# Skip term and gate of a state-space stage per chunk, and its last branch products per half of their inputs

## What is computed

```python
cum = jnp.cumsum(ai, axis=1)                      # scan over chunks, forward and backward
y = jnp.einsum('btsg,btsge,bsgep->btgep', cb, Lm, xi)
y = y + jnp.einsum('btgn,bgenp->btgep', ci, S) * jnp.exp(cum)[..., None]
S_new = jnp.exp(cum[:, -1])[..., None, None] * S + jnp.einsum(...)
...
o_b = o_b + lp['d_skip'].reshape(SSM_GROUPS, SSM_HPG, 1) * xh      # the skip term
o_b = o_b.reshape(Bn, L, SSM_INNER) * jax.nn.silu(z)               # the gate
o_b = rms_norm_3(o_b.reshape(Bn, L, SSM_GROUPS, 512), norm_w)      # needs all of a group
y_b = o_b @ lp['w_pb']
merged = jax.nn.sigmoid(gate_a) * y_a + jax.nn.sigmoid(gate_b) * y_b
```

## Time and profile before

| | |
|---|---|
| median of 3 runs | 3487.12 us (3480.87 to 3489.39) |
| the profiled execution | 3491.64 us, of which its span is 3489.6 us |
| PE, DVE, POOL, ACT busy | 93%, 61%, 39%, 36% of the span |
| the stage | 2712 to 3054 us of the span |
| groups 0 to 3, end of the last `out` | 2773.1, 2857.9, 2927.3, 2999.7 us |

### The profile page before, as it was taken

The page is one execution under the profiler, slowest core; times in us unless marked ns, Lnnn a source line. Parts: engine busy times, 40 slices in busy tenths (PEclk is TensorE's granted clock), DMA queues, the critical chain, the costliest instruction groups (busy, mean ns, idle before and its releaser), DMA issues. The chain is left out here.

```text
span 3489.6 us, 44690 instructions
## 1 busy us (share of the span) xinstructions
PE 3258.9 (93%) x17806; PEld 2622.1 (75%) x17806; DVE 2117.2 (61%) x2504; ACT 1249.0 (36%) x1899; POOL 1371.3 (39%) x625
## 2 busy tenths in 40 slices
PE   8999998999998998999999999888989868899998
PEld 6778777888866677977888877767877646678886
DVE  6586865889865476354756554868982777631112
ACT  4233343323344332333423342334441654332222
POOL 3434343444432233435344433326641322334443
PEclk9999999999999999999999999999999979999999
DMA  3223353465333245444444222533333755422322
GB/s 120 91 85 125 123 172 131 168 233 179 132 113 97 79 132 156 129 164 156 148 145 151 96 98 88 176 97 125 105 113 115 231 156 151 154 85 83 106 92 76
DMA packets 237662, 451.26 MB, mean 129 GB/s; under 512 B 59936, under 2 KB 120032, under 8 KB 230416
## 3 DMA queue, kind: packets, MB, share of 16 engines
q1 hardware_dynamic: 230384, 437.93, 38.8%
q10 hardware_dynamic: 7072, 10.49, 0.8%
HBM read 396.88 MB, written 51.46 MB: 128 GB/s over the span
## 5 line engine op out<-in xcount | busy, mean ns | idle before, releaser
L288 POOL TENSOR_TENSOR stream_feed_lo<-stream_feed_raw,stream_feed_hi 128x1024 fp32r<-128x1024 f32 (+4 forms) x555 | 1255.8, 2265 | 2013.4 <-ACT stream_feed_hi L281 1959.5
L281 ACT ACTIVATE stream_feed_hi<-stream_feed_raw 128x1024 fp32r<-128x1024 f32 (+4 forms) x555 | 533.3, 963 | 707.5 <-PE ffn_low L188 174.9
L186 PE MATMUL shared_ps<-third_h_hi,stream_feed_hi 128*128 128x512 f32 (+1 forms) x776 | 322.1, 415 | 39.2 <-ACT third_in_rows_bend L794 17.1
L187 PE MATMUL shared_ps<-third_h_lo,stream_feed_hi 128*128 128x512 f32 (+1 forms) x776 | 311.3, 401 | 0.0
L188 PE MATMUL shared_ps<-third_h_hi,stream_feed_lo 128*128 128x512 f32 (+1 forms) x776 | 311.3, 401 | 0.0
L186 PE MATMUL mixer_acc<-first_h_hi,stream_feed_hi 128*128 128x512 f32 x544 | 222.2, 408 | 7.2 <-DVE first_h_lo L1406 5.4
L480 DVE SCALAR_TENSOR_TENSOR ffn_ada_sum<-ffn_ada_w,cond,ffn_ada_sum 128x512 f32<-128x512 f32 x196 | 219.0, 1134 | 4.1
L186 PEld LDWEIGHTS shared_ps<-third_h_hi,stream_feed_hi 128*128 128x128 f32 (+1 forms) x776 | 151.1, 195 | 85.6 <-issue 44.3
L188 PE MATMUL mixer_acc<-first_h_hi,stream_feed_lo 128*128 128x512 f32 x544 | 214.2, 394 | 0.0
L187 PE MATMUL mixer_acc<-first_h_lo,stream_feed_hi 128*128 128x512 f32 x544 | 214.1, 394 | 0.0
L186 PE MATMUL ffn_low<-ffn_mid_hi,stream_feed_hi 128*128 128x512 f32 x528 | 207.6, 393 | 4.7 <-DVE x_res L702 4.6
(11 more groups left out here) (767 smaller groups left out, 7243.0 us busy)
## 6 DMA issues: line engine op xcount, KB each, us to landing
stream_feed_raw<-in_stream SPq DMA_DIRECT2D x406, 512.0 KB, 3.4
ffn_ada_w<-in_w_ada SPq DMA_DIRECT2D x48, 1024.0 KB, 5.4
stream_feed_raw<-in_stream SPq DMA_DIRECT2D x50, 384.0 KB, 3.1
stream_feed_raw<-in_stream SPq DMA_DIRECT2D x52, 256.0 KB, 3.0
stream_feed_raw<-in_stream SPq DMA_DIRECT2D x36, 320.0 KB, 3.0
scratch_gates<-mixer_gate ACTq DMA_DIRECT2D x32, 256.0 KB, 2.1
mix_gin<-scratch_gates SPq DMA_DIRECT2D x32, 256.0 KB, 3.2
x_res<-scratch_cum SPq DMA_DIRECT2D x16, 512.0 KB, 7.6
```

What stands on the lines that cost most here:

```text
L186: nc.tensor.matmul(out, w_hi, x_hi, start=start, stop=False)
L187: nc.tensor.matmul(out, w_hi, x_lo, start=False, stop=False)
L281: self.nc.scalar.activation(self.hi[:, p % self.cut, :n], self.raw[:, p % self.deep, :n], ACT.Copy).then_inc(self.cut_hi, 1)
L288: eng.tensor_tensor(self.lo[:, p % self.cut, :n], self.raw[:, p % self.deep, :n], self.hi[:, p % self.cut, :n].bitcast(F32), ALU.subtract) ...
```

## The change

The skip term and the gate are done for chunk c of all four tiles at once: four instructions of 128 columns and one of 512, on data that `load_gate` fetches as 128 positions of 512 channels. On DVE, chunks 0 to 2 follow `out(g, 1)` to `out(g, 3)`, and chunk 3 closes the group. SP loads chunk 2 after e6 and chunk 3 after the next group's first `load_e`. `square` comes earlier on ACT, and `sums` on PE ahead of the six products. The last eight pieces become four pieces with the first half of the inputs of two column blocks each, and four with the second; eight sums are open at once, in eight banks, and the evictions follow `closed` (even blocks) or the spent piece (odd ones). SP loads all remaining weight pieces ahead of the gate rows. The diff, cut to its core:

```diff
@@ -3775,14 +3775,15 @@
-        self.cut, self.lesser, self.freed, self.gated = (s.sem(n) for n in ("cut", "lesser", "freed", "gated"))
+        self.cut, self.lesser, self.freed, self.gated, self.closed = (
+            s.sem(n) for n in ("cut", "lesser", "freed", "gated", "closed"))
...
-        return self.acc[:, q % 4 if q >= 2 * DT else q % 2]
+        return self.acc[:, (0, 1, 2, 3, 4, 6, 7, 5)[q - 2 * DT] if q >= 2 * DT else q % 2]

@@ -3814,34 +3815,30 @@
-    def tensor_last(self, pe, some, sums):
...
+    def tensor_last(self, pe, freeing, sums, before_sums):
+
+        def halves(part, m):
+            if m % 2 == 0:
+                self.w[0] = self.feed.take(pe, *self.pieces[2 * DT + DT // 2 * part + m // 2])
+            w_hi, w_lo = self.w[0]
             for k in range(DT // 2):
+                at, of = DT // 2 * part + k, DT // 2 * (m % 2) + k
+                if m == 0:
+                    self.wait_input(pe, 2 * DT, at)
+                last = product(self.nc, self.bank(2 * DT + m), (w_hi[:, of], w_lo[:, of]),
+                               (self.h[0][:, at], self.h[1][:, at]), at == 0, at == DT - 1)
+            if m % 2:
+                self.feed.spent(last)
+            elif part:
+                last.then_inc(self.closed, 1)
+
+        for m in range(DT):
+            if m == before_sums:
                 sums()
+            freeing(m)
+            halves(0, m)
+        for m in range(DT):
+            halves(1, m)

@@ -3865,7 +3862,13 @@
     def vector(self, dve, done):
         v = self.nc.vector
         for q in range(self.evicted, done):
-            self.feed.done(dve, *self.pieces[q])
+            m = q - 2 * DT
+            if m < 0:
+                self.feed.done(dve, *self.pieces[q])
+            elif m % 2:
+                self.feed.done(dve, *self.pieces[2 * DT + DT // 2 + m // 2])
+            else:
+                dve.wait_ge(self.closed, m // 2 + 1)
             dve.wait_ge(self.gate_in[q % 2], 16 * (q // 2 + 1))
             if q > DT:
                 dve.wait_ge(self.gated, q - DT)
@@ -3894,7 +3897,7 @@
-        y, xg, z = s.sb("y", [P, 4, T]), s.sb("xg", [P, 2, T]), s.sb("z", [P, 2, T])
+        y, xg, z = s.sb("y", [P, 4, T]), s.sb("xg", [P, 2, 4, P]), s.sb("z", [P, 2, 4, P])
@@ -3963,21 +3966,18 @@
-                def load_gate(g, j):
-                    n = 4 * g + j
+                def load_gate(g, c):
+                    n = 4 * g + c
                     if n >= 2:
                         sp.wait_ge(gated, n - 1)
-                    sp.dma_start(xg[:, j % 2], dram["xbc"][n * P:(n + 1) * P]).then_inc(xz_in[j % 2], 16)
-                    sp.dma_start(z[:, j % 2], dram["z"][Z3["z"] + n * P:Z3["z"] + (n + 1) * P]
-                                 ).then_inc(xz_in[j % 2], 16)
+                    for to, at in ((xg, dram["xbc"][T * g:T * (g + 1)]),
+                                   (z, dram["z"][Z3["z"] + T * g:Z3["z"] + T * (g + 1)])):
+                        sp.dma_start(to[:, c % 2], rows(at)[:, :, c * P:(c + 1) * P]).then_inc(xz_in[c % 2], 16)

                 for g in range(4):
                     dense.sync_gates(sp, pieces_by(g - 1, 1, 2) if g else 0)
                     dense.sync(sp, before(g, 0))
-                    if g:
-                        for j in range(2, 4):
-                            load_gate(g - 1, j)
-                    else:
+                    if g == 0:
                         load_x(0, 2)
                         load_x(0, 3)
                     for n in range(6, 8):
@@ -4004,6 +4004,7 @@
                     load_e(g, 6)
+                    load_gate(g, 2)
                     for n in range(2, 4 if g < 3 else 0):
                         load_cum(g + 1, n)
                     load_e(g, 7)
@@ -4012,15 +4013,16 @@
                         for n in range(4, 6):
                             load_cum(g + 1, n)
                         load_start(g + 1)
-                        for n in range(3):
-                            load_e(g + 1, n)
-                for j in range(2, 4):
-                    load_gate(3, j)
+                        load_e(g + 1, 0)
+                    load_gate(g, 3)
+                    for n in range(1, 3 if g < 3 else 0):
+                        load_e(g + 1, n)
                 sp.wait_ge(intra_ready, 28)
                 sp.dma_start(core.x[:], dram["x_keep"]).then_inc(x_back, 16)
+                dense.sync_gates(sp, 2 * DT)
+                dense.sync(sp, 3 * DT)
                 for q in range(2 * DT, 3 * DT):
                     dense.sync_gates(sp, q)
-                    dense.sync(sp, q)
                 sp.wait_ge(x_back, 16)

@@ -4089,6 +4091,9 @@
                         if j == 1:
                             fill(g, 0, 1)
                     fill(g, 0, 2)
+                    if g:
+                        pe.wait_ge(x_scaled, 8 * g + 8)
+                        sums(g - 1)
                     for n in range(6):
@@ -4100,8 +4105,6 @@
                             pe.wait_ge(advanced, 6 * g + n - 1)
-                        if n == 1 and g:
-                            sums(g - 1)
                         if d:
                             fill(g, 0, 3 + n // 2)
                     for c in range(4):
@@ -4132,8 +4135,20 @@
                         fill(g, 1, c)
-                pe.wait_ge(read, 30)
-                dense.tensor_last(pe, 1, lambda: (pe.wait_ge(y_made, 16), sums(3)))
+
+                def freeing(m):
+                    if m < 2:
+                        pe.wait_ge(dense.freed, 2 * DT - 1 + m)
+                    if m == 2:
+                        pe.wait_ge(read, 30)
+                    if m == 3:
+                        pe.wait_ge(read, 31)
+                    if m == 5:
+                        pe.wait_ge(y_made, 16)
+                    if m == 7:
+                        pe.wait_ge(meaned, 4)
+
+                dense.tensor_last(pe, freeing, lambda: (pe.wait_ge(y_made, 16), sums(3)), 2)

@@ -4151,8 +4166,8 @@

                 def square(g):
                     act.wait_ge(inter_ready, 4 * g + 4)
+                    act.wait_ge(gated, 4 * g + 4)
                     for j in range(4):
-                        act.wait_ge(gated, 4 * g + j + 1)
                         a.activation(squares[j], y[:, j], ACT.Square).then_inc(squared, 1)

                 def root(g):
@@ -4180,11 +4195,11 @@
                     for n in range(2 if g == 0 else 0):
                         decay(0, n)
                     dense.scalar(act, before(g, 0))
+                    if g:
+                        square(g - 1)
                     for n in range(2 if g == 0 else 3, 4):
                         decay(g, n)
                     dense.scalar(act, pieces_by(g, 0, 0))
-                    if g:
-                        square(g - 1)
                     dense.scalar(act, pieces_by(g, 0, 1))
                     for n in range(4, 6):
                         decay(g, n)
@@ -4201,8 +4216,9 @@
                         dense.scalar(act, pieces_by(g, 1, k))
                         if g < 3:
                             decay(g + 1, k)
+                dense.scalar(act, 2 * DT)
                 square(3)
-                dense.scalar(act, 2 * DT)
+                dense.scalar(act, 2 * DT + 1)
                 root(3)
                 high_parts(3)
                 for q in range(2 * DT, 3 * DT):
@@ -4225,15 +4241,15 @@
-                def gate(g, some):
-                    for j in some:
-                        n = 4 * g + j
-                        dve.wait_ge(y_made, 4 * g + 4)
-                        dve.wait_ge(xz_in[j % 2], 32 * (n // 2 + 1))
-                        v.scalar_tensor_tensor(out=y[:, j], in0=xg[:, j % 2], scalar=core.v("d_skip", n), in1=y[:, j],
-                                               op0=ALU.mult, op1=ALU.add).then_inc(skipped, 1)
-                        dve.wait_ge(skipped, n + 1)
-                        v.tensor_tensor(y[:, j], y[:, j], z[:, j % 2], ALU.mult).then_inc(gated, 1)
+                def gate(g, c):
+                    n, part = 4 * g + c, y[:, :, c * P:(c + 1) * P]
+                    dve.wait_ge(y_made, n + 1)
+                    dve.wait_ge(xz_in[c % 2], 32 * (n // 2 + 1))
+                    for j in range(4):
+                        v.scalar_tensor_tensor(out=part[:, j], in0=xg[:, c % 2, j], scalar=core.v("d_skip", 4 * g + j),
+                                               in1=part[:, j], op0=ALU.mult, op1=ALU.add).then_inc(skipped, 1)
+                    dve.wait_ge(skipped, 4 * n + 4)
+                    v.tensor_tensor(part, part, z[:, c % 2], ALU.mult).then_inc(gated, 1)

@@ -4307,8 +4323,6 @@
                     dense.vector(dve, before(g, 0))
-                    if g:
-                        gate(g - 1, (0, 1))
                     dve.wait_ge(grammed, g + 1)
                     if g:
                         dve.wait_ge(masked[0], 4 * g)
@@ -4328,8 +4342,6 @@
                         if j == 1:
```

(52 more changed lines are left out.)

## The result

The changed kernel takes 3511.47 us (median; 3509.45 to 3514.07), the kernel before in the same session 3487.78. The ratio is 1.0069, 95% interval 1.0056 to 1.0081: slower by 23.7 us. The prediction had 3506.5, and the measured time is inside its range.

What follows compares the result with a forecast made beforehand. PE, busy 93% of the span, was taken as the bound, so only its idle time could change. Terms 7.0 + 6.5 - 1.3 - 3.0 + 10.2 = +19.4 on 3491.64 gave 3511.0; median 4.5 lower, 3506.5; range 3495 to 3518.

Steps and rivals of the forecast that it cites:

- the five terms: Groups 0-1 +7.0, 1-2 +6.5, 2-3 -1.3, end of group 3 -3.0, behind PE's last product +10.2 us.
- chunk 3 in time: Rival at the load queue: chunk 3 lands before DVE needs it, +3, 3490 us; chance 0.10.
- the end covered: Rival at the stage's end: gate rows 18 to 23 come early, last term nil, +9, 3496 us; chance 0.08.
- The lock: Rival: DVE's chunk gates slowed beside POOL in the loops, five on the path adding 11 us, 3517; chance 0.05.
- Behind the last product: Stage end: gate rows queued behind all weight pieces delay six sums, last addition 11.6 us after PE; net +10.2.
- The end of group 3: DVE-bound end of group 3: fourth gate and sums end earlier, PE's last product 3049.6 instead of 3052.6; -3.
- The sign that the prediction gave for this place: If right, PE's last product would come some 3 us earlier relative to the last `out`.
- Group 2 into 3: Between groups 2 and 3: weighing starts at 2945.5 instead of 2946.78, two gates ahead of it gone; -1.3 us.
- The price of a transfer: Load queue: 512 KB costs 2.35 us in 512 B runs, 1.48 in 2 KB runs, for each `xg` and `z` pair.
- e7: Last e tile loaded in a group; group 0's was to land at 2775.0, where the row says 2770.97.
- Group 0 into 1: Between groups 0 and 1: DVE waits 5.7 us for chunk 3, all of group 1 queues behind; `invert` +7 us.
- group 1 into 2: Between groups 1 and 2: same late chunk 3, sums ahead of the products on the path; `invert` +6.5 us.

Runs made afterwards that it cites:

- E1: Changed kernel with gate rows 18 to 23 issued between the last weight pieces instead of behind all of them: 3503.62 us, ratio 1.0046.
- E2: Changed kernel with chunk 3's gate data issued right behind the group's last e tile, ahead of the next group's tiles: 3499.01 us, ratio 1.0033.
- E4: Changed kernel with gate transfers reading 2 KB rows instead of 512-byte runs, same bytes and order, wrong blocks computed: 3516.09 us, ratio 1.0078.
- E9: Changed kernel with the edits of E1 and E2, sums behind the first two products, and chunk 2 also behind e7: 3484.19 us, ratio 0.9987.
- E11: E9 with cum tile 3 of the next group moved from ahead of e7 to behind the gate chunks: 3480.09 us, ratio 0.9973.
- E12: Kernel before with only the chunk gates, chunks 2 and 3 right behind e7, sums behind two products, old end: 3489.73 us, ratio 0.9999.
- E10: Kernel before with only the new last products and weight layout, gate rows 18 to 23 between the last weight pieces: 3486.10 us, ratio 0.9986.

## Why the prediction was right, and where its steps failed

**The direction and the places** were right: the five terms stand where they were put, with their signs, and each of the two large losses fell away when its cause was taken out (E1, E2). The rivals with chunk 3 in time and with the end covered fell in the first profile. The lock came, at another place than that rival had it: the chunk gates take 1.13 or 1.14 us everywhere, but the weighing and the steps of the state now meet POOL's work. In group 3 the weighing took 6.54 us for three tiles where the earlier trace rows have 1.89; in the kernel before, two later instructions of that group had paid about as much (2.15 and 2.84 instead of 0.69), so that the increment is still -0.7. In group 2 one instruction pays on the path, as told below.

**Behind the last product (+10.2, measured +10.5).** The chain of piece, split, issue and landing was right: the first row was there 2.2 us after PE's end (forecast 1.9), and the six sums took 9.8 us from then (forecast 9.7).

**The end of group 3 (-3, measured -2.4).** The sums there took 4.6 us, 3019.60 to 3024.20, where the forecast had 3.6. The sign that the prediction gave for this place, PE's last product 3 us earlier against the last `out`, does not follow from its own sum, which gives 5.2 (`y` 2.2 us later, PE 3.0 earlier); 5.2 is what was measured.

**Group 2 into 3 (-1.3, measured -0.7)** was right within what one trace can tell.

**The price of a transfer** was wrong in its cause. From rates of 212 and 354 GB/s I made the length of the runs the reason; E4 changes that length alone and finds 0.24 us a pair at most; E1, whose loads there are those of the changed kernel, has a share of 72.2%, so that most of even this is what differs between two profiles. By the Trainium skill (DMA: Bandwidth & Descriptors, Specifications) runs from 512 bytes on move at line rate. The shares of E4 (71.7% against 73.2% for the same bytes) are nearer to that than to the 0.87 us of the prediction, which weighed it wrongly. What else makes the queue slow at 2845 was not tried. And the stretch from which the 2.35 us were taken was not all queue: SP stood at e7's buffer from 2763.13 to 2765.05, and the share of the whole stretch is 0.83.

```profile
2760.38:2770.97 10.59, 10.59 (x107) 9.55 (x107) 8.47 (x10) 10.49 (x28) 2.99 (x2) 1.00 0.83 204
```

**Yet e7 and chunk 3 came as late as forecast**, on the clock of before e7 at 2775.8 (forecast 2775.0) and chunk 3 at 2785.5 (2784.7). For e7 that was luck. By the wrong price the first `cum` tile was to come 1.7 us later than before; it came 0.5 later (40.02 us after the first `cb`, 39.53 before). What the forecast had not counted is SP's hold of 2.35 us at chunk 2's buffer, which kept back the two `cum` tiles ahead of e7 while the queue ran nearly empty. One error stood in for the other; the rule "where the change adds a wait, name what is queued behind it" had been kept for DVE and not for SP. With chunk 2 ahead, e7 of group 0 is first used 52.8 to 55.0 us after the first `cb`; with it behind, 51.1 to 52.4 and without a wait (E9, E11, E12); in the kernel before it was 50.1. How much of this is the hold and how much chunk 2's bytes is not shown: these kernels move both, and SP issues e7 no earlier in E9 (45.64 us after the first `cb`) than in the changed kernel (45.74).

**Group 0 into 1 (+7, measured +10.8) and group 1 into 2 (+6.5, measured +8.6)** were undersized, in the terms of PE and by one of DVE. In the first, chunk 3's gate ends 0.75 us later than forecast; the twelve products cost 1.0 more than "say 4", the six products 0.9 more, the sums 4.36 instead of 3.6: 3.4 in all. PE ran the twelve products at a granted clock of 0.53 behind 7.3 us of idle time, and the six products and the sums at 0.64 and 0.79 behind another 2.1. I had bounded one of these terms by half clock and taken the rest from rows at 1.00, though the forecast itself had made PE idle there.

In the second, `xdt` ends 1.7 us earlier than forecast (e7 came 0.8 us later than before there, for the forecast 2.35). The sums cost 1.6 more, at 0.68 behind 11.65 us of idle time. The last 2.2 us lie between the sums and `invert`, and were in no term: one step of the state on DVE, with both inputs in SBUF, took 2.83 us beside POOL's multiplication where its like takes 0.68. The first line here is the weighing ahead of it, which the sums cover. Timelines of DVE and POOL:

```profile
2879.43 4.05 DVE L4232 TENSOR_TENSOR ssm_xw<-ssm_xdt,ssm_w 128x512 f32<-128x512 f32 x3
...
2886.87 2.83 DVE L4232 TENSOR_TENSOR shared_states<-shared_states,third_ecum 128x512 f32<-128x512 f32 x1
...
2886.38 2.77 POOL L4033 TENSOR_TENSOR shared_seg<-shared_seg,ssm_cb 128x1024 f32<-128x1024 f32 x1 [4.06 <-ACT shared_seg L4165]
```

These terms are why the sum was +19.4 and the stage lost +26.8.

## What to carry to other kernels

In a queue written out by hand, a load that is moved has two prices: the bytes ahead of what follows, and its own wait for a buffer, which holds everything behind it; count both for SP as for DVE. Finer chunks win nothing by themselves. Here the change is 0.7% slower with chunk 3 and six gate rows at the back of their lists. With the loads in the order of their use, the chunks alone are level with the kernel before (E12), the new tail alone is 0.1% faster (E10), and both together, with the sums put back behind two products, 0.1 to 0.3% (E9, E11). After an idle time that a forecast gives to PE, the next work should be priced from rows at the lower clock. And where work is taken out of one engine's list, look at what the rest of that list then runs beside: here it was the weighing beside POOL.

## What was not expected of the hardware

E1 has evictions early enough to run beside POOL's split of the next weights, and three of its additions on DVE (both inputs in SBUF) took 2.56, 1.95 and 2.63 us instead of 0.69, one of them in the rows of E1 above; E10 shows 2.61, 1.95 and 2.58. It costs little there, since the last two additions take 0.69 and the last ends 1.8 us behind PE. It is the behaviour of the earlier trace rows at a place where the kernel before had at most 0.96. And the same instructions ahead of the stage took up to 11 us more or less from one profile to the next, 0.3% of the span, which is why all small differences here are counted from an instruction inside the trace.
